# Two plain column blocks and 28 Strassen pairs in the up projection, and the last tile stored in four pieces by two queues

## The reference

```python
mod = c_act @ w_ada[l] + b_ada[l]          # six shifts, scales and gates
h = rms_norm(x, g_pre_attn[l]) * (1.0 + sc_a) + sh_a
proj = h @ w_in[l]
...                                        # two head groups of attention, normalised and joined
o = o @ w_out[l]
x = x + gt_a * rms_norm(o, g_post_attn[l])

h = rms_norm(x, g_pre_mlp[l]) * (1.0 + sc_m) + sh_m
y = jnp.square(jax.nn.relu(h @ w_mlp_in[l])) @ w_mlp_out[l]
x = x + gt_m * rms_norm(y, g_post_mlp[l])
```

## Time and profile before

| what | value |
|---|---|
| median of 3 runs | 2043.9 us (2042.99 to 2044.48) |
| the profiled execution, its own time | 2043.85 us |
| its span in the trace | 2042.2 us |
| PE busy | 2006.2 us, 98% of the span |
| DVE busy | 1715.3 us, 84% |
| ACT busy | 992.3 us, 49% |
| POOL busy | 158.5 us, 8% |
| chain that ended last, by engine | PE 93%, DVE 3%, ACT 2%, issue 1% |
| plain blocks in the trace | 748.73 to 884.92 us |
| Strassen pairs in the trace | 884.92 to 1409.3 us |

### The profile page before, as it was taken

One profiled execution on the slowest core, in us unless ns is written; L12 is line 12 of the kernel. 1 busy time (PEld: TensorE's weight loads), 2 busy tenths in 40 slices (PEclk: granted clock), 3 DMA queues, 4 the chain that ended last, 5 costly groups with the idle time before them and its releaser, 6 DMA issues.

```text
span 2042.2 us, 30709 instructions
## 1 busy us (share of the span) xinstructions
PE 2006.2 (98%) x11141; PEld 1751.4 (86%) x11141; DVE 1715.3 (84%) x1998; ACT 992.3 (49%) x1399; POOL 158.5 (8%) x170
## 2 busy tenths in 40 slices
PE   6999999999999999999999999999999999999998
PEld 6888888878888878899999999999788888888886
DVE  5986898877877777699999999988898898898866
ACT  5454322578833365455665656565333333333322
POOL 0000000057610000000000000000200000000000
PEclk8999999999999999999999999999999999999999
DMA  8997868710187754766666676768757457457452
GB/s 296 342 297 249 282 206 235 217 64 1 52 294 252 227 185 123 246 212 229 217 221 216 221 227 215 232 205 314 267 193 264 168 185 267 165 186 265 168 182 83
DMA packets 295660, 432.28 MB, mean 212 GB/s; under 512 B 30196, under 2 KB 180504, under 8 KB 286744
## 3 DMA queue, kind: packets, MB, share of 16 engines
q1 hardware_dynamic: 278056, 361.43, 53.5%
q0 software_dynamic: 15936, 63.97, 8.5%
q10 hardware_dynamic: 1584, 5.77, 0.8%
HBM read 367.15 MB, written 63.96 MB: 211 GB/s over the span
## 4 chain that ended last, share of the span: by engine, by line
PE 93%; DVE 3%; ACT 2%; issue 1%; DMA 0%; SPq 0%; ACTq 0%; DVEq 0%
PE bank L2937 9%; PE bank L2939 9%; PE bank L2938 9%; PE bank L2915 9%; PE bank L2917 9%; PE bank L2916 9%; PE bank L2425 6%; PE bank L2427 6%; PE bank L2426 6%; PE bank L2438 2%; PE bank L2440 2%; PE bank L2439 2%; PE bank L3000 1%; PE bank L2999 1%; PE bank L2998 1%
## 5 line engine op out<-in xcount | busy, mean ns | idle before, releaser
L1401 ACT ACTIVATE hi<-w 128x1024 fp32r<-128x1024 f32 x168 | 178.4, 1063 | 264.8 <-PE bank L2939 197.9
L2937 PE MATMUL bank<-hi,y_use 128*128 128x512 f32 x784 | 306.6, 391 | 0.0
L2938 PE MATMUL bank<-lo,y_use 128*128 128x512 f32 x784 | 305.1, 389 | 0.0
L2939 PE MATMUL bank<-hi,y_use 128*128 128x512 f32 x784 | 305.1, 389 | 0.0
L864 ACT ACTIVATE hi<-raw 128x1024 fp32r<-128x1024 f32 (+2 forms) x128 | 128.3, 1012 | 281.0 <-DMA raw<-in_w_in 107.6
L1320 ACT ACTIVATE hi<-a 128x1024 fp32r<-128x1024 f32 x182 | 191.9, 1054 | 142.1 <-DVE a L2129 129.5
L2126 DVE TENSOR_TENSOR lo<-a,hi 128x1024 fp32r<-128x1024 f32 x182 | 221.9, 1219 | 41.1 <-ACT hi L1320 40.7
L2915 PE MATMUL bank<-h_hi,hi 128*128 128x256 f32 x832 | 235.6, 283 | 0.0
L2917 PE MATMUL bank<-h_hi,lo 128*128 128x256 f32 x832 | 235.5, 283 | 0.0
L2916 PE MATMUL bank<-h_lo,hi 128*128 128x256 f32 x832 | 235.5, 283 | 0.0
L2241 DVE TENSOR_TENSOR lo<-w,hi 128x1024 fp32r<-128x1024 f32 x168 | 205.1, 1227 | 31.2 <-ACT hi L1401 30.8
(11 more groups left out here) (390 smaller groups left out, 4701.6 us busy)
## 6 DMA issues: line engine op xcount, KB each, us to landing
raw<-in_w_ada SPq DMA_DIRECT2D x166, 512.0 KB, 5.1
w<-in_w_mlp_out SPq DMA_DIRECT2D x128, 512.0 KB, 4.8
y_use<-y_dram SPq DMA_DIRECT2D x53, 1024.0 KB, 9.2
a<-in_w_mlp_in SPq DMA_DIRECT2D x104, 512.0 KB, 4.5
y_dram<-y_out POOLq DMA_DIRECT2D x28, 1792.0 KB, 6.8
raw<-in_w_in SPq DMA_DIRECT2D x32, 512.0 KB, 5.7
raw<-in_w_out SPq DMA_DIRECT2D x32, 512.0 KB, 4.6
gate_row<-in_w_ada SPq DMA_DIRECT2D x26, 512.0 KB, 5.2
```

The source lines that it names most:

```text
L2937: mm(bank[b + m][:], yh, hi[s][:, q, :], start=j == 0, stop=False)
L2938: mm(bank[b + m][:], yh, lo[s][:, q, :], start=False, stop=False)
L2939: ins = mm(bank[b + m][:], yl, hi[s][:, q, :], start=False, stop=j == PAIRS - 1)
```

## The change

It does six things.

- `PLAIN_BLOCKS` is 2: the plain part has 16 units in place of 24, and 28 pairs go through the seven products.
- The preparation of the Strassen operands is moved: its steps stand at units 6 to 9 and 11 to 13 in place of 7 to 10 and 16 to 18, and ACT's three rounds at units 10 to 12 in place of 13 to 15. The gate's rows stand after units 6, 10, 14 and 15; two of six go over to the added Strassen pairs.
- The bank sets of the plain blocks are exchanged (`up_set`), and with them the banks of the transposes, of the filler matmuls and of the last squares ahead of the up projection.
- ACT's scaling of the third tile's last 1536 columns stands behind the second column of h.
- At the end POOL adds up the squares of the first three column blocks for all four tiles; the root takes the last block's sum and that value itself, and DVE's reduce and division for each tile are gone.
- The last tile is stored as 1024, 512, 384 and 128 columns: the first and the third by SP, the second and the fourth by ACT. DVE adds the last 512 columns in two pieces.

```diff
-PLAIN_BLOCKS = 3
+PLAIN_BLOCKS = 2
-GATE_AFTER = (6, 8, 14, 15, 18, 21)
+GATE_AFTER = (6, 10, 14, 15)
...
+        up_set = lambda f: sets[(PLAIN_BLOCKS - 1 - f) % 2]
...
-                for first, blocks in ((0, 2), (2, 2)) if t < NT - 1 else ((0, 2), (2, 1), (3, 1)):
+                for first, blocks in ((0, 2), (2, 2)) if t < NT - 1 else ((0, 2),):
...
-            sp.wait_ge(out_saved, 16 * (2 * NT + 1))
+            sp.wait_ge(out_ready, NB * NT)
+            sp.dma_start(out_d[NT - 1][:, D - COLS:D - P], x1_back[NT - 1][:, D - COLS:D - P]).then_inc(out_saved, 16)
+            sp.wait_ge(out_saved, 16 * (2 * NT + 2))
...
-                if t >= 2:
-                    act.wait_ge(row_done, (NB - 1) * 4 + t - 1)
-                nc.scalar.activation(bank[3 * (t % 2)][:], part[:, t, :], ACT.Square, accum_out=row_sq[:, t, NB - 1:NB]).then_inc(row_done, 1)
+                nc.scalar.activation(bank[4 + t][:], part[:, t, :], ACT.Square, accum_out=row_sq[:, t, NB - 1:NB]).then_inc(row_done, 1)
...
-            scale_x1(NT - 2, slice(COLS, D), xn_rest)
             for k in range(KD):
...
+                if k == 1:
+                    scale_x1(NT - 2, slice(COLS, D), xn_rest)
...
-                    if 13 <= j < 16:
-                        round_t(1, *((t_one, one_f[1]), (t_three, three_f[1]), (t_two, two_f[1]))[j - 13])
+                    if 10 <= j < 13:
+                        round_t(1, *((t_one, one_f[1]), (t_three, three_f[1]), (t_two, two_f[1]))[j - 10])
...
             def final_root(t):
-                act.wait_ge(y_var, t + 1)
-                nc.scalar.activation(stat_s[:, t, 2:3], stat_v[:, t, 2:3], ACT.Sqrt).then_inc(y_sqrt, 1)
+                act.wait_ge(y_var, 1)
+                act.wait_ge(y_sq, NT * (NB - 1) + t + 1)
+                nc.scalar.activation(stat_s[:, t, 2:3], row_sq[:, t, NB - 1:NB], ACT.Sqrt, scale=1.0 / D, bias=stat_v[:, t, 2:3]).then_inc(y_sqrt, 1)
...
+            for n, cols in ((NB * NT - 1, slice(D - 2 * COLS, D - COLS)), (NB * NT + 1, slice(D - P, D))):
+                act.wait_ge(out_ready, n)
+                act.dma_start(out_d[NT - 1][:, cols], x1_back[NT - 1][:, cols]).then_inc(out_saved, 16)
...
-            T_STEPS = {7: [lambda: join(one_f[0], h_12)], 8: [lambda: join(one_f[1], h_11)], 9: [made_one, lambda: join(three_f[0], h_22)],
...
+            T_STEPS = {6: [lambda: join(one_f[0], h_12)], 7: [lambda: join(one_f[1], h_11), made_one],
+                       8: [lambda: join(three_f[0], h_22), made_three], 9: [made_two], 11: [lambda: t_low(1, t_one, one_f[1])],
...
-                own.step(nc.vector.tensor_reduce(stat[:, t, 2:3], row_sq[:, t, :], AX.X, ALU.add))
-                ts(stat_v[:, t, 2:3], stat[:, t, 2:3], 1.0 / D, EPS, ALU.mult, ALU.add).then_inc(y_var, 1)
...
+                    for e in ((0, COLS - P), (COLS - P, COLS)) if (t, n) == (NT - 1, NB - 1) else ((0, COLS),):
+                        to = x1_back[t][:, n * COLS + e[0]:n * COLS + e[1]]
+                        stt(to, z[:, e[0]:e[1]], rstd[:, t, 2:3], to, ALU.mult, ALU.add).then_inc(out_ready, 1)
...
-                    ins = turn_x1(k, t, bank[4 + k])
+                    ins = turn_x1(k, t, bank[k])
...
-                            pe.wait_ge(relu_done, 8)
+                            pe.wait_ge(relu_done, 4 * (PLAIN_BLOCKS - 1))
...
-            up_block(1)
-            pe.wait_ge(relu_done, 4)
             pair_block()
...
+            rest = stat_v[:, :, 2:3]
+            pool.wait_ge(y_sq, NT * (NB - 1))
+            own.step(tt(rest, row_sq[:, :, 0:1], row_sq[:, :, 1:2], ALU.add))
+            own.step(tt(rest, rest, row_sq[:, :, 2:3], ALU.add))
+            nc.gpsimd.tensor_scalar(rest, rest, 1.0 / D, EPS, ALU.mult, ALU.add).then_inc(y_var, 1)
```

More of the change, by code:

```diff
@@ L2831, in _ @@
                 if t == NT - 1:
+                    pe.wait_ge(row_done, (NB - 1) * 4 + 1)
                     for i in range(12):
-                        mm(bank[1][:], o_hi[:, KD - 1, 0:P], o_hi[:, KD - 1, :], start=True, stop=True)
+                        mm(bank[4][:], o_hi[:, KD - 1, 0:P], o_hi[:, KD - 1, :], start=True, stop=True)
                 pe.wait_ge(xn_ready, t + 1)
@@ L2849, in first_columns @@
                 pe.wait_ge(h2_hi_done, 1)
+                out = up_set(0)
                 for n in range(4):
-                    mm(bank[n][:], hi[s][:, 0, n * P:(n + 1) * P], h2_hi[:, 0, :], start=True, stop=False)
-                    mm(bank[n][:], lo[s][:, 0, n * P:(n + 1) * P], h2_hi[:, 0, :], start=False, stop=False)
+                    mm(out[n][:], hi[s][:, 0, n * P:(n + 1) * P], h2_hi[:, 0, :], start=True, stop=False)
+                    mm(out[n][:], lo[s][:, 0, n * P:(n + 1) * P], h2_hi[:, 0, :], start=False, stop=False)
                 pe.wait_ge(h2_ready, 1)
                 for n in range(4):
-                    mm(bank[n][:], hi[s][:, 0, n * P:(n + 1) * P], h2_lo[:, 0, :], start=False, stop=False)
+                    mm(out[n][:], hi[s][:, 0, n * P:(n + 1) * P], h2_lo[:, 0, :], start=False, stop=False)
                 pe.wait_ge(h2_ready, 2)
@@ L2858, in first_columns @@
                     wh, wl = hi[s][:, 1, n * P:(n + 1) * P], lo[s][:, 1, n * P:(n + 1) * P]
-                    mm(bank[n][:], wh, h2_hi[:, 1, :], start=False, stop=False)
-                    mm(bank[n][:], wh, h2_lo[:, 1, :], start=False, stop=False)
-                    ins = mm(bank[n][:], wl, h2_hi[:, 1, :], start=False, stop=False)
+                    mm(out[n][:], wh, h2_hi[:, 1, :], start=False, stop=False)
+                    mm(out[n][:], wh, h2_lo[:, 1, :], start=False, stop=False)
+                    ins = mm(out[n][:], wl, h2_hi[:, 1, :], start=False, stop=False)
                 ins.then_inc(w_used, 1)
@@ L2871, in pair_block @@
                     for n in range(2):
-                        out = sets[0][2 * pr + n][:]
+                        out = up_set(PLAIN_BLOCKS - 1)[2 * pr + n][:]
                         for q in range(4):
```

18 lines of the change are left out of this document (7 added, 11 removed).

## The result

Twelve runs of each kernel: the changed kernel takes 2046.38 us in the median (2044.36 to 2048.66), the kernel before 2043.09 us (2041.25 to 2045.50). The ratio is 1.0015, with a 95% interval of 1.0008 to 1.0022: slower by 3.1 us (1.6 to 4.5). The profiled execution took 2047.49 us with a span of 2045.8 us, 3.6 us over the span profiled before; it is 1.1 us slower than the median.

What follows compares the result with a forecast made beforehand. TensorE was taken to bound the plain blocks and Strassen pairs, with VectorE, ScalarE and the last store at the end. Terms -3.2 - 0.7 + 5.9 - 0.4 = +1.6 us gave 2045.5 us, range 2041.5 to 2048.0.

Steps and rivals of the forecast that it cites:

- Blocks, -3.2: Column blocks: one plain block of 43.52 us goes, two pairs of 20.16 us come; TensorE's work falls by 3.20 us.
- Front, -0.7: Up projection's start: first h about 0.9 us earlier, ahead of ScalarE's scaling, 0.2 lost again; gain 0.7 us.
- Wait at the third product, 4.5: First Strassen pair: TensorE waits 4.5 us for ScalarE's snapshot, since VectorE's operand work has fewer plain units beside it.
- ScalarE's chain: First pair, from VectorE's mix to the first product's snapshot: 6.7 us, with hand-overs 6.9.
- VectorE's walk: VectorE's queue from unit 6's split to the third pair's mix: 57.1 us plus holes of 1.0 and 0.9, sum 59.0.
- the landing of the first sum's load: Weights for the first Strassen sum: landing taken at 5.5 us after issue, median 6.2; uncertainty 0 to +1.8 us.
- Wait at the seventh, 1.5: First pair's seventh product: VectorE's second corner 1.5 us late, against 0.14 before.
- rival 3: Wait at the third product halves TensorE's clock; 10 us of it gives +5.1 us, 2049.0 us; chance 0.10.
- The Trainium skill's rule: TensorE's clock returns after one busy window, so the half-speed stretch vanishes in the seventh product's wait; forecast unchanged.
- End, -0.4: Last token tile: shorter root chain gains 0.4 us, between 0.9 gained and 0.2 lost; four store pieces cost nothing.
- No wait: First Strassen pair: VectorE keeps up and TensorE doesn't wait; -4.3 us, 2039.6 us; chance 0.09.
- half a wait: First Strassen pair: half the wait, ScalarE or the holes going better; about 2042.3 us; chance 0.13.

Runs made afterwards that it cites:

- both kernels with the steps on GpSimd: Last two steps of the seventh product's operand moved from VectorE to GpSimd, in the changed kernel's order (1.0033) and in a repaired reordering of VectorE and ScalarE (1.0008).
- the mended order: Changed kernel with first two Strassen pairs' work reordered on ScalarE and VectorE, a first reordering repaired: 0.9996; here also with two operand steps on GpSimd: 1.0008.

## Why the prediction was right, and where its terms were off

The forecast was 2045.5 us, +1.6; measured +3.1 (1.6 to 4.5), inside the range and within 0.2% of the kernel before. Of the 1.0 us between the forecast and the +2.6 of the stretches that belong to the change, 0.7 are in the first pair's wait, 0.4 in the front, and the end gives 0.2 back. Step by step:

- **Blocks, -3.2.** Seen -3.14 (plain blocks -43.46, pairs +40.32). Right.
- **Front, -0.7.** The mechanism is right: 0.9 us at full clock (0.62 against the kernel with the blocks alone), of which the plain blocks lose 0.05 to 0.12 again and not 0.2. That the fillers may run at half clock and take 0.6 of it back was not in the sum: the exchange of banks and fillers was costed at nothing because the order of waits stays. So it is -0.8 in most traces and -0.3 in the changed kernel's.
- **Wait at the third product, 4.5.** Seen 5.05 (5.21 late). The place, the releaser and the chain are as told; ScalarE's chain is 6.34 us as read from the earlier trace rows. VectorE's walk took 60.0 us where the forecast had 59.0; its two holes were 1.01 and 0.71 us (forecast 1.0 and 0.9). The term that was too small is the landing of the first sum's load, which I took at 5.5 us. It was 6.2, the median of the earlier trace rows, and VectorE stood 0.77 us for it. Work put there won 0.5 us of the wait back, about what the forecast missed.
- **Wait at the seventh, 1.5.** Seen 0.06, but the clock cost 1.50 us at the third product in its place, which the text had under rival 3 as the case that changes nothing. With the clock held up the seventh product was 1.40 late. The term was right as a sum and not as the place; that the clock cost so nearly the same is partly luck, since in another execution the third product lost 2.30 us to it, some 0.6 more than the wait that it replaced. The Trainium skill's rule that stands beside rival 3 (TensorE: Matmul & The Clock Gate, Part 1: The HAM clock gate) had the same outcome for the changed kernel, and its trace agrees, with 3.2 us of work at half clock.
- **End, -0.4.** Seen -0.57, and 0.56 to 0.60 in every kernel with the new end. The four pieces were not quite free: from the first issue of the last tile until SyncE goes on behind the last landing are 4.28 us (2037.69 to 2041.78 before, 4.09). Of these 0.19 us, 0.13 are that the last piece is issued 1.46 us after the first and not 1.32; whether the second queue costs anything of its own is not shown.
- **Rivals.** No wait and half a wait are out: the wait was longer than the forecast's. The low clock came, for 3.4 us, and cost what it replaced in the changed kernel's trace.

What stays open: 0.5 us between the sum of the stretches without the two terms that are not of the change (+2.6) and the measured ratio (+3.1), which lies inside the interval; and which executions get the front at full clock, and how many the longer stretch at half.

## What to carry to other kernels

A step taken off the busiest engine also takes away the time in which another engine did its unrelated work; walk that engine's queue over the new span before counting the gain. A wait that is removed by moving one instruction shows up at the next consumer of the same late engine, so test a suspected cause by taking work off that engine, not by moving the instruction that is waited for. Before handing work from VectorE to GpSimd, look whether VectorE has work with two operands to do meanwhile.

## What was not expected of the hardware

- GpSimd's additions of 128x2048 (4.60 and 5.44 us) held VectorE's instructions with two operands until they were over, 1.23 us becoming 4.79.
- After idle times of much the same length (5.05 and 4.54 us) TensorE's clock stayed at 0.50 for 3.2 us of work in one execution and for 5.0 in another. An idle time of 2.60 us brought it down too, in both kernels with the steps on GpSimd (0.50 from 841.00 to 844.41 in the mended order, with work again from 841.43). The fillers ahead of the up projection ran at full clock in eight executions and at half in four.
- A product that starts after a wait takes 2.94 to 2.98 instead of 2.88 us at full clock, so that a wait costs about 0.1 us more than it lasts.
